# One step of a hybrid decoder trunk on one core: roots and reciprocals of all norms on sums laid out by token quarters

## What is computed

```
def _rms_norm(x, g):
    xf = x.astype(jnp.float32)
    y = xf * lax.rsqrt(jnp.mean(xf * xf, axis=-1, keepdims=True) + EPS) * g.astype(jnp.float32)
    return y.astype(x.dtype)
...
        h = _rms_norm(x, p["norm_mix"][i])
        ...
            q = _rope(_rms_norm(q, p["q_norm_att"][j]), pos)
            k = _rope(_rms_norm(k, p["k_norm_att"][j]), pos)
        ...
        qx = _rms_norm(qx.reshape(n, t, N_X_HEADS, HEAD_DIM), p["q_norm_x"][i])
        o_x = _cross_attend(qx, mem_k[i], mem_v[i]).reshape(n, t, X_DIM)
        o = jnp.concatenate([o_self, o_x.astype(o_self.dtype)], axis=-1)
        x = x + o @ p["w_out"][i]
        hm = _rms_norm(x, p["norm_mlp"][i])
        x = x + jnp.square(jax.nn.relu(hm @ p["w_up"][i])) @ p["w_down"][i]
```

## Time and profile before

| | |
|---|---|
| median of 3 runs | 1253.14 us (1251.64 to 1256.35) |
| profiled execution | 1250.36 us, of it the span from first to last instruction 1248.6 us |
| mean granted clock of TensorE | 0.987 |
| busy: TensorE, VectorE, ScalarE, GpSimd | 97%, 47%, 32%, 20% |
| memory stage | 0 to 58 us |
| attention projection | 58 to 137 us |
| attention | to 231 us |
| output projection and first MLP | 231 to 671 us |
| convolution stage | 671 to 811 us |
| output projection and second MLP | to the end |

### The profile page before, as it was taken

How to read it: one execution, slowest core, us unless ns; L and a number is a source line. 1 busy time by engine, 2 the same in 40 slices (tenths; PEclk the granted TensorE clock), 3 DMA queues, 4 the chain that set the end, 5 groups by cost and what they waited for, 6 DMA issues and landing times.

```text
span 1248.6 us, 21831 instructions
## 1 busy us (share of the span) xinstructions
PE 1208.0 (97%) x9436; PEld 1166.3 (93%) x9436; DVE 583.5 (47%) x716; ACT 397.0 (32%) x578; POOL 244.0 (20%) x231
## 2 busy tenths in 40 slices
PE   4899798999999999999999999999999999999998
PEld 4899555899999999999999999999999999999998
DVE  7899653445333433433446644655432433333341
ACT  7332575424313213312322222333421321321320
POOL 7736786340000000000042212233000000000000
PEclk9999888999999999999999999999999999999999
DMA  7434321222231322222121322222222132232221
GB/s 274 167 113 115 126 102 68 102 102 70 100 102 68 102 89 80 91 77 101 67 101 68 146 83 73 74 70 100 76 94 102 69 102 98 70 101 69 99 91 48
DMA packets 22853, 120.16 MB, mean 96 GB/s; under 512 B 2676, under 2 KB 6644, under 8 KB 9732
## 3 DMA queue, kind: packets, MB, share of 16 engines
q1 hardware_dynamic: 17892, 100.93, 23.5%
q0 software_dynamic: 1632, 10.54, 2.3%
q10 hardware_dynamic: 3264, 7.74, 1.8%
HBM read 111.29 MB, written 5.69 MB: 94 GB/s over the span
## 4 chain that ended last, share of the span: by engine, by line
PE 86%; DVE 8%; POOL 4%; issue 1%; DMA 1%; ACT 1%; ACTq 0%; DVEq 0%; POOLq 0%
PE zps L410 80%; POOL sm L1223 3%; DVE tmp L718 2%; DVE w_lo L693 2%; PE ops L576 1%; PE ops L544 1%; PE tps L516 1%; DVE act_lo L837 1%; DMA tmp<-z 1%; DVE act_lo L733 0%; DVE z L703 0%; PE zps L474 0%; PE ops L560 0%; DVE rstd L710 0%; PE zps L480 0%
## 5 line engine op out<-in xcount | busy, mean ns | idle before, releaser
L410 PE MATMUL zps<-act_hi,w_hi 128*128 128x272 f32 (+1 forms) x2880 | 608.1, 290 | 2.5 <-DVE w_lo L849 2.2
L410 PE MATMUL zps<-act_hi,w_lo 128*128 128x272 f32 (+1 forms) x2880 | 602.1, 289 | 0.0
L410 PE MATMUL zps<-act_lo,w_hi 128*128 128x272 f32 (+1 forms) x2880 | 600.4, 288 | 0.0
L410 PEld LDWEIGHTS zps<-act_hi,w_hi 128*128 128x128 f32 x2880 | 457.2, 189 | 7.5 <-DVE w_lo L849 2.9
L410 PEld LDWEIGHTS zps<-act_lo,w_hi 128*128 128x128 f32 x2880 | 456.5, 189 | 0.1
L410 PEld LDWEIGHTS zps<-act_hi,w_lo 128*128 128x128 f32 x2880 | 453.6, 189 | 0.0
L693 DVE TENSOR_TENSOR w_lo<-w_stage,w_hi 128x2048 fp32r<-128x2048 f32 x91 | 216.8, 2382 | 127.5 <-ACT w_hi L951 127.3
L951 ACT ACTIVATE w_hi<-w_stage 128x2048 fp32r<-128x2048 f32 (+1 forms) x93 | 175.6, 1889 | 277.4 <-PE zps L410 249.7
L741 DVE TENSOR_TENSOR x_res<-zps,x_res 128x544 f32<-128x544 f32 x80 | 57.9, 724 | 226.7 <-PE zps L410 225.9
L1056 ACT ACTIVATE tmp<-tmp 128x544 f32<-128x544 f32 x64 | 42.3, 660 | 246.9 <-DVE tmp L815 246.9
L815 DVE SCALAR_TENSOR_TENSOR tmp<-zps,rstd 128x544 f32<-128x544 f32 x64 | 46.2, 722 | 152.5 <-PE zps L410 152.4
(11 more groups left out here) (115 smaller groups left out, 526.8 us busy)
## 6 DMA issues: line engine op xcount, KB each, us to landing
w_stage<-wst SPq DMA_DIRECT2D x92, 1024.0 KB, 4.9
kx<-xkT POOLq DMA_DIRECT2D x4, 1024.0 KB, 5.2
vx<-xv POOLq DMA_DIRECT2D x4, 1024.0 KB, 7.1
x_res<-xT ACTq DMA_DIRECT2D x1, 2176.0 KB, 11.1
tmp<-z ACTq DMA_DIRECT2D x32, 68.0 KB, 2.0
yT<-x_res ACTq DMA_DIRECT2D x8, 272.0 KB, 2.1
memx<-memT SPq DMA_DIRECT2D x2, 512.0 KB, 4.6
vb<-swav POOLq DMA_DIRECT2D x1, 1024.0 KB, 7.8
```

The source lines that it names most:

```text
L410: mm = pe.matmul(zps[slot][:, h, 0:n], w_[:, d, k, w:w + 128], r_[:, k, c0 + h * n:c0 + (h + 1) * n], start=(j == 0 and i == 0), stop=(j = ...
```

## The change

The sums of all norms are laid out differently for root and reciprocal. Four matmuls with 32 output columns each put the sum of the four quarters of the tokens into the four groups of 32 partitions of tps, so 136 columns hold all 544 (64 hold 256). In a group, 16 partitions hold the sum of one head and 16 that of the other; for the token norms all 32 hold the same. Root and reciprocal work on these 136 columns. Then four matmuls with a 0/1 selector (64 rows each, two row halves by two) bring the reciprocals back to all partitions and 544 columns, in tps. For the token norms VectorE copies them to rstd. The head norms' product reads them out of tps.

The order changes with it. TensorE's spread stands in the middle of the panel that follows the sum (midway, after the fourth of eight chunks). VectorE's short reciprocal stands right behind the take of the panel and so ahead of the split and of the low part of the norm (head_inverse, token_inverse). The tile tps is now free for the next sum only when the product or copy has read it. The constants grow from 256 to 320 columns for the matrices. The declarations of the new semaphores are left out here.

```diff
@@ -53,9 +53,9 @@
 C_SINK = C_CW + 18
 C_SROW = C_SINK + 12
 C_IDENT = C_SROW + 4
-C_ONES = C_IDENT + 128
-C_HEAD = C_ONES + 128
-C_MASKP = C_HEAD + 128
+C_SEL = C_IDENT + 128
+C_SUM = C_SEL + 256
+C_MASKP = C_SUM + 64
 C_MASKS = C_MASKP + 256
 C_BLK = C_MASKS + 132
 C_ST = C_BLK + 2 * SB
@@ -167,8 +167,7 @@
         y_out, st_rdy = sem("y_out"), sem("st_rdy")
 
         ident = con[:, C_IDENT:C_IDENT + 128]
-        ones = con[:, C_ONES:C_ONES + 128]
-        headones = con[:, C_HEAD:C_HEAD + 128]
+        head_sum, token_sum = con[:, C_SUM:C_SUM + 32], con[:, C_SUM + 32:C_SUM + 64]
         eps = con[:, C_EPS:C_EPS + 1]
 
         def gain(norm, k):
@@ -182,6 +181,9 @@
 
         def halves(ap2d):
             return ap2d.rearrange("p (h t) -> p h t", h=2)
+
+        def wide(ap2d, cols):
+            return ap2d[:, 0:cols].rearrange("p (h t) -> p h t", h=2)
 
         def zp(slot, n=HALF):
             return zps[slot][:, :, 0:n]
@@ -415,27 +417,50 @@
                     if between is not None:
                         between(j, mm)
 
+            def quarter_sums(kind, src, cols):
+
+                w = cols // 4
+                for j in range(4):
+                    mm = pe.matmul(tps[32 * j:32 * j + 32, 0, 0:w], kind, src[:, j * w:(j + 1) * w], start=True, stop=True)
+                return mm
+
+            def spread_quarters(cols):
+
+                w = cols // 4
+                for i in range(2):
+                    for half in range(2):
+                        r = slice(64 * half, 64 * half + 64)
+                        mm = pe.matmul(tps[:, half, i * w:(i + 1) * w], con[r, C_SEL + 128 * i:C_SEL + 128 * (i + 1)],
+                                       tmp[r, 3, 0:w], start=True, stop=True)
+                return mm
+
             def colsum(n, cols):
-
                 pe.wait_ge(sq_acc, n)
                 take(tfree)
-                parts = 2 if cols > 512 else 1
-                w = cols // parts
-                for h in range(parts):
-                    mm = pe.matmul(tps[:, h, 0:w], ones, pacc[:, h * w:(h + 1) * w], start=True, stop=True)
-                mm.then_inc(s_full, 1)
-                tfree[0] = (s_sd, n)
+                quarter_sums(token_sum, pacc, cols).then_inc(s_full, 1)
+
+            def colspread(n, cols):
+                pe.wait_ge(s_inv, n)
+                spread_quarters(cols).then_inc(s_spread, 1)
+                tfree[0] = (s_rstd, n)
 
             def headsum(n):
-
                 pe.wait_ge(n_sq, n + 1)
                 take(tfree)
-                parts = 2 if norm_cols(n) > 512 else 1
-                w = norm_cols(n) // parts
-                for h in range(parts):
-                    mm = pe.matmul(tps[:, h, 0:w], headones, tmp[:, n % 2, h * w:(h + 1) * w], start=True, stop=True)
-                mm.then_inc(n_ms, 1)
-                tfree[0] = (n_sd, n + 1)
+                quarter_sums(head_sum, tmp[:, n % 2, :], norm_cols(n)).then_inc(n_ms, 1)
+
+            def headspread(n):
+                pe.wait_ge(n_inv, n + 1)
+                spread_quarters(norm_cols(n)).then_inc(n_spread, 1)
+                tfree[0] = (n_out, n + 1)
+
+            def midway(*calls):
+
+                def between(j, mm):
+                    if j == KC // 2 - 1:
+                        for f, args in calls:
+                            f(*args)
+                return between
 
             def turn_memv(n):
                 l, c = n // 2, n % 2
@@ -600,7 +625,8 @@
             def mlp_group(q, l, u0, first=None, stat=None):
 
                 for m in range(8):
-                    panel(q + m // 4, m % 4, *act_hl[1 - l], ready=first if m == 0 else None)
+                    panel(q + m // 4, m % 4, *act_hl[1 - l], ready=first if m == 0 else None,
+                          between=midway((colspread, (stat, NT))) if m == 1 and stat else None)
                     if m == 0 and stat:
                         colsum(stat, NT)
                 for m in range(8):
@@ -620,8 +646,9 @@
             colsum(1, NMEM)
             for l in range(2):
                 for p in range(4):
+                    mid = [(colspread, (1, NMEM))] if (l, p) == (0, 0) else [(headspread, (2 * l + p - 2,))] if p >= 2 else []
                     panel(Q_MEM + l, p, *act_hl[1], l * NMEM, (l + 1) * NMEM,
-                          ready=(lambda k: (m_los[l], k + 1)) if p == 0 else None, guard=l > 0 or p >= 2)
+                          ready=(lambda k: (m_los[l], k + 1)) if p == 0 else None, guard=l > 0 or p >= 2, between=midway(*mid))
                     if p in (1, 2):
                         headsum(2 * l + p - 1)
                     if p == 3:
@@ -630,7 +657,8 @@
                         turn_memv(1)
 
             for i in range(12):
-                panel(Q_ATT + i // 4, i % 4, *act_hl[0], ready=normed(0) if i == 0 else None)
+                mid = [(colspread, (2, NT))] if i == 1 else [(headspread, (N_ATT + i - 2,))] if i >= 2 else []
+                panel(Q_ATT + i // 4, i % 4, *act_hl[0], ready=normed(0) if i == 0 else None, between=midway(*mid))
                 if i == 0:
                     turn_memv(3)
                     colsum(2, NT)
@@ -657,8 +685,9 @@
 
 
             for i in range(20):
+                mid = [(colspread, (4, NT))] if i == 1 else [(headspread, (N_QX[1] + i - 2,))] if i in (2, 3) else []
                 panel(Q_CONV + i // 4, i % 4, *act_hl[1], ready=normed(2) if i == 0 else None,
-                      between=between_sx if i == at_s(J_SX[1]) + 4 else chunk_read if i == 19 else None)
+                      between=between_sx if i == at_s(J_SX[1]) + 4 else chunk_read if i == 19 else midway(*mid))
                 if i == 0:
                     colsum(4, NT)
                 if i in (1, 2):
@@ -705,21 +734,29 @@
                     ins = dve.tensor_tensor(out, zps[p % 2][:, 0, 0:cols], rstd[:, 0:cols], ALU.mult)
                 ins.then_inc(z_free[p % 2], 1)
 
-            def inv_rms(n, cols):
+            def token_inverse(n, cols):
                 dve.wait_ge(s_sd, n)
-                dve.reciprocal(rstd[:, 0:cols], tmp[:, 2, 0:cols]).then_inc(s_rstd, 1)
+                dve.reciprocal(tmp[:, 3, 0:cols // 4], tmp[:, 2, 0:cols // 4]).then_inc(s_inv, 1)
+
+            def token_rstd(n, cols):
+                dve.wait_ge(s_spread, n)
+                dve.tensor_copy(wide(rstd, cols), tps[:, :, 0:cols // 2]).then_inc(s_rstd, 1)
                 dve.wait_ge(s_rstd, n)
+
+            def head_inverse(n):
+                cols = norm_cols(n)
+                dve.wait_ge(n_sd, n + 1)
+                dve.reciprocal(tmp[:, 3, 0:cols // 4], tmp[:, 2, 0:cols // 4]).then_inc(n_inv, 1)
 
             def head_norm(n):
                 kind, l, i = NORMS[n]
                 cols = norm_cols(n)
-                dve.wait_ge(n_sd, n + 1)
+                dve.wait_ge(n_spread, n + 1)
                 taken(dve, *norm_panel(n))
-                link(dve.reciprocal(tmp[:, 3, 0:cols], tmp[:, 2, 0:cols]))
                 src = norm_src(n)
                 dst = memk[:, l, i, :] if kind == "mem" else src
-                dve.scalar_tensor_tensor(out=dst, in0=src, scalar=hgain(norm_gain(n)), in1=tmp[:, 3, 0:cols],
-                                         op0=ALU.mult, op1=ALU.mult).then_inc(n_out, 1)
+                dve.scalar_tensor_tensor(out=wide(dst, cols), in0=wide(src, cols), scalar=hgain(norm_gain(n)),
+                                         in1=tps[:, :, 0:cols // 2], op0=ALU.mult, op1=ALU.mult).then_inc(n_out, 1)
 
             def turned_memv(n):
                 l, c = n // 2, n % 2
@@ -809,7 +846,8 @@
                     split_next(q + m // 4, m % 4)
                     full(dve, q + m // 4, m % 4)
                     if m == 0 and stat:
-                        inv_rms(stat, NT)
+                        token_inverse(stat, NT)
+                        token_rstd(stat, NT)
                     if m >= 2 or not first:
                         dve.wait_ge(u_sq, u0 + (m - 1))
                     dve.scalar_tensor_tensor(out=halves(tmp[:, m % 2, :]), in0=zp(m % 2), scalar=0.0,
@@ -848,14 +886,17 @@
                 c = slice(half * 128, half * 128 + 128)
                 dve.tensor_tensor(w_lo[:, 0, :, c], stage[:, 0, :, c], w_hi[:, 0, :, c].bitcast(f32), ALU.subtract).then_inc(done, 1)
             link(dve.tensor_scalar(nsink[:, :], con[:, C_SINK:C_SINK + 16], -1.0, None, ALU.mult))
+            token_inverse(1, NMEM)
             split_lo(0, 1)
-            inv_rms(1, NMEM)
+            token_rstd(1, NMEM)
             for l in range(2):
                 for p in range(4):
                     q = Q_MEM + l
                     if (l, p) != (0, 0):
                         split_next(q, p)
                     take_scaled(q, p, tmp[:, 4 + p // 2, (p % 2) * 256:(p % 2) * 256 + 256], NMEM)
+                    if p in (1, 2):
+                        head_inverse(2 * l + p - 1)
                     norm_lo(0, 4 * l + p, 0)
                     if p in (1, 2):
```

(28 more changed lines are left out.)

## The result

The changed kernel took 1267.42 us (median of 4, 1265.62 to 1273.67), the kernel before 1252.97 on the same chip: a ratio of 1.012, 95% interval 1.0079 to 1.0161. It is slower, by 14.5 us where 3 were forecast, and outside the range of 1250 to 1264. The profiled execution took 1265.62 us with a span of 1263.8.

A forecast was written before the change was run, and what follows sets the result against it. TensorE was taken to bound the kernel, busy 97% of the span. +1.5 us through the attention stage and +1.35 behind it make about +2.9; with the median 2.8 above the profiled run, 1256 us, range 1250 to 1264.

The forecast's parts named there:

- The part on the rest: Behind the attention: three token norms and two head norms cost TensorE +1.35 us; shortened reciprocals and larger constants give nothing.
- the slower one: Rival: short reciprocals come late, so TensorE stops mid panel in some ten panels; 1262 us, chance 0.22.
- Price of a norm on TensorE: Quarter sum 0.49 and spread 0.69 us replace a 0.92 us product: 0.27 us more per norm, seven attention panels 50.4 us.
- The lower bound: If small matmuls ran fully side by side, only columns would count: 0.68 us per norm, 0.24 less than before.
- VectorE: Short reciprocal 0.99 us, product 0.75, token copy 0.72; 2.6 us shed per head norm, no TensorE wait in attention panels.
- VectorE's lag of 3.1 us: Behind attention panel 9: the lag goes and no more is gained, since TensorE sets the pace; take at 123.8.
- Swap and burst: End of attention: swap issued 0.4 us earlier, output burst 2.0 later; +1.5 us up to here, TensorE restarts at 145.6.
- The term of +2.0 for the burst: End of attention: if the swap's landing follows the end of the output transfers' burst, the stage loses 2.0 us.
- Memory stage: From 0 to 58 us: first attention panel starts 0.5 us later, range 0 to +2.
- The stalls ahead of the spreads: Memory stage, middle of panel 3 of each half: TensorE waits for the reciprocal, two new stalls of about 2 us.

The follow-up runs named there:

- e1: The changed kernel with 24 idle waiting instructions added at TensorE's start, so both loops begin 24 instructions later: 1257.17 us, ratio 1.0032 to the kernel before.
- e2: The kernel before with 172 idle TensorE instructions ahead of the first loop, which then begins at place 193: 1264.97 us, ratio 1.0103.
- e3: The changed kernel with 24 idle TensorE instructions at the start and 24 more ahead of the convolution, second loop at 193: 1271.23 us, ratio 1.0155.
- h2: The kernel before with the new layout only for token norms 1 and 2, four memory-stage head norms and the attention projection's last three: 1248.93 us, ratio 0.9968.
- t1: The kernel before with memory and attention stage reciprocals cut to a quarter of their columns (wrong results), TensorE's program untouched: 1243.46 us, ratio 0.9928.
- h3: The kernel before with the new layout only for token norms 1 and 2 and the memory stage's four head norms, plus 32 waiting instructions: 1251.74 us, ratio 1.0013.
- h1: The changed kernel with the old full products for the three token norms and two head norms behind the attention: 1255.27 us, ratio 1.0017.

## Why the prediction was wrong

**The step that failed: the program's own place had no term.** The part on the rest counts the new matmuls by their time alone and closes with "The constants grow by 64 columns, 32 KB; nothing". The 428 instructions ahead of the first loop stand nowhere. They moved the loop from place 21 to 193, and that cost two branches back with a refetch, 7.0 us each: 14 of the 15.2 us between the spans. e1, e2 and e3 show it from three sides: gone with 24 more instructions, made in the kernel before by 172, moved to the other loop by 24. No rival held it; the slower one, at 1262, was about a wait that no trace shows. Nothing in the profile of before could have put a chance on 193, but a look at TensorE's two loops could have put a rival there, with some 1 in 12 for each loop (21 of 256).

The other steps, beside e1 where the gaps matter:

- **Price of a norm on TensorE.** Predicted 0.27 us, seven panels 50.4 us. Measured 0.50 and 52.1 (72.02 to 124.09). The timeline of TensorE around a spread shows what was missing:

```profile
75.26 0.41 PE L412 MATMUL zps<-act_hi,w_lo 128*128 128x272 f32 x2
75.60 0.73 PE L433 MATMUL tps<-tmp,con 64*128 64x136 f32 x8
76.27 0.52 PE L412 MATMUL zps<-act_hi,w_hi 128*128 128x272 f32 x2
76.62 0.41 PE L412 MATMUL zps<-act_lo,w_hi 128*128 128x272 f32 x2
```

By the prediction's own way of reading (from the small product's start to the second pair behind it, less 0.25) the spread takes 0.77 us (predicted 0.69), and the sum, from 72.02 to 72.75, 0.48 (0.49). That way starts too late: the small product begins 0.34 us after the pair ahead of it, where pairs follow each other at 0.25, and so does the sum. These two steps make 0.18 us, the spread 0.08. In the chain the same shows as 3.20 instead of 3.00 us for each half of a panel. The lower bound, by columns alone, was far off.
- **VectorE.** The reciprocal 1.00 us, the product 0.78, the copy 0.72 as said. The take of panel 9 came right at its end, and no attention panel waited for a reciprocal. Right. (In h2 the first short reciprocal stands behind a full norm on VectorE, and its spread waited 0.68 us.)
- **The gain that was eaten.** VectorE's lag of 3.1 us went, and TensorE's panels grew by 3.5: the take is at 124.20 for 124.21. t1 has what the lag and the memory stage were worth without TensorE's part, 8.7 us. From 8.7 faster to 3.8 slower are 12.5 us for 21 norms, 0.6 each, and by the estimate at equal clock 11.1 us, 0.5 each, which is the price above: TensorE's price ate it. That is a mean over all 21; the price of a norm in the memory stage wasn't measured by itself.
- **Swap and burst.** Issued at 125.10 (I had 124.7) and landed at 134.92. The term of +2.0 for the burst was wrong: SP issued o_mk at 122.34, 1.6 later than before, and the swap landed 0.2 sooner. h2 agrees; t1 can't tell, since its burst came sooner too (o_mk at 114.42). The restart came at 143.50 instead of 145.6.
- **Memory stage.** Predicted +0.5; in the changed kernel's profile it is -1.3. The stalls ahead of the spreads were 0.8, 0.2 and 1.1 us, not two of 2. But in e1 the same code began the attention at 53.26, 1.3 later than before, since 36 matmuls that took 4.49 us in the changed kernel's profile took 6.82. Most of them started 0.21 us apart instead of 0.12. That is the pace of the kernel before from 39.7 to 42.7 us, where its granted clock had fallen (0.66 from 40 to 44); for this early stretch of e1 the profile's clock reads 1.00, so here the lower clock is inferred. The median of h3, which is about this stage, shows no difference, and at equal clock it is 1.9 us slower. So the sign stays open; the size is about 1 us.
- **The rest.** Predicted +1.35 us for five norms. From the output projection to the end e1 needs 1020.0 us, the kernel before 1017.6: +2.4, 0.48 each. The same missing 0.2 as above. Their reciprocals gave nothing, as said.

With the place out of it, the change costs 3.8 us by medians (4.9 at equal clock) where the sum said 2.9, and the forecast of 1256 would have come near e1's 1257.17. Part of that is luck, for the two misses in the sum pull apart: the burst's 2.0 us weren't there, and a norm costs 0.2 us more than its price.

## What to carry to other kernels

Where an engine's loop is long (here 1558 instructions), any edit ahead of the loop can cost or save several us that have nothing to do with the edit. Compare the packets of the instruction queue and look for gaps named "issue" at the loop's period before crediting the change, and time the edit again with a few idle instructions ahead of the loop (24 were enough here).

A shorter operation on an engine that isn't the bound is worth its lag, once: here 3.1 us, at the last panel. Pay for it only there (h2, three norms of ten, 2.8 us under h3), not in every panel.

A product in another shape costs the products around it too: read the price from the period of the loop, or from the matmul ahead of it to the one behind, not from its own row.

## What the runs showed of the hardware

- A branch back that fetches again costs 4.5 to 4.75 us of standing at place 193 (the changed kernel, e2, e3) and then some 2.3 us at the lower granted clock. The two of them bring 17 packets of 16 KB more (33 for 16 in e1, from 229 to 670 us). By the block size of the page cited above the body fills seven or eight, so it seems to be fetched whole, one packet in the gap and the rest under the work. At the good places no packet comes in groups 2 and 3: the body is kept.
- It depends on the place of the loop: 185 and 193 of 256 stall, 177 and 201 don't, and at 185 the gap is in two parts. Why the zone is where it is, these runs don't say, since the start of the count is unknown.
- TensorE's pace at the start of the kernel differs between executions: the first panel's last 36 matmuls took 4.49, 6.09, 6.58, 6.78 and 6.82 us in five kernels with the same code there (the changed one, h2, h3, h1, e1), and the attention began up to 2.6 us apart. It is as large as the effects studied, which is why single profiles were used for places and medians for sizes.
- 0.01 of mean granted clock goes with about 6 us of this kernel's time. Two medians a few us apart are best compared together with the clocks of their executions.
